# Keys and values of the memory tokens: computed in the first stage and kept in a DRAM buffer, instead of computed between the two blocks

## The reference, cut to what matters

```
def memory_mixer(q, mem, mem_norm_g, w_mem_kv):
    kv = (rmsnorm(mem, mem_norm_g) @ w_mem_kv).reshape(b, mem.shape[1], 2, MEM_HEADS, MEM_DH)
    k, v = kv[:, :, 0], kv[:, :, 1]
    ...
```

## Time and profile before

| | |
|---|---|
| median of three runs | 2339.71 us |
| the profiled execution (its span; no other time of it was kept) | 2339.5 us |
| PE busy | 2263.0 us, 97% of the span |
| DVE busy | 1471.0 us, 63% |
| ACT busy | 1038.2 us, 44% |
| POOL busy | 45.4 us, 2% |
| moved by DMA | 458.63 MB, mean 196 GB/s |
| GB/s in the first slices of 58.5 us | 367, 372, 146, 196 |
| chain that ended last | PE 86%, DVE 5%, ACT 2%, DMA 2% |

### The profile page before, as it was taken

One profiled execution on the slowest core, in us unless ns is written; L12 is line 12 of the kernel. 1 busy time (PEld: TensorE's weight loads), 2 busy tenths in 40 slices (PEclk: granted clock), 3 DMA queues, 4 the chain that ended last, 5 costly groups with the idle time before them and its releaser, 6 DMA issues.

```text
span 2339.5 us, 37594 instructions
## 1 busy us (share of the span) xinstructions
PE 2263.0 (97%) x15609; PEld 2029.3 (87%) x15609; DVE 1471.0 (63%) x2074; ACT 1038.2 (44%) x1429; POOL 45.4 (2%) x57
## 2 busy tenths in 40 slices
PE   5899999999999999989999999999999999999997
PEld 2577788899888999779999988999978998999986
DVE  3346766488476479766888855566665544576664
ACT  3134233354555643344444433444454434454444
POOL 2000000021000000000000000000000000000000
PEclk9899999999999999999999999999999999999999
DMA  9946666455444578866778756666646466644464
GB/s 367 372 146 196 219 206 200 149 151 150 126 136 127 186 243 282 290 225 198 226 248 256 228 189 190 184 181 185 184 162 192 148 192 195 175 130 131 134 198 144
DMA packets 249610, 458.63 MB, mean 196 GB/s; under 512 B 18931, under 2 KB 43825, under 8 KB 248032
## 3 DMA queue, kind: packets, MB, share of 16 engines
q1 hardware_dynamic: 246496, 442.47, 60.5%
q0 software_dynamic: 2368, 9.56, 1.1%
q10 hardware_dynamic: 576, 4.19, 0.5%
HBM read 454.07 MB, written 2.10 MB: 195 GB/s over the span
## 4 chain that ended last, share of the span: by engine, by line
PE 86%; DVE 5%; ACT 2%; DMA 2%; DVEq 2%; issue 1%; SPq 1%; ACTq 0%
PE psum L639 76%; DVE fast L1912 1%; DVE sbuf L1960 1%; DMA sbuf<-in_w_ada 1%; PE psum L616 1%; ACT fast L1315 1%; PE psum L1041 1%; PE psum L1148 1%; PE psum L710 1%; PE psum L892 1%; PE psum L947 1%; DVEq L1959 1%; PE psum L966 1%; PE psum L1178 1%; SPq L510 1%
## 5 line engine op out<-in xcount | busy, mean ns | idle before, releaser
L639 PE MATMUL psum<-fast,fast 128*128 128x256 f32 (+3 forms) x13440 | 2037.5, 312 | 19.3 <-DVE fast L1912 13.3
L639 PEld LDWEIGHTS psum<-fast,fast 128*128 128x128 f32 (+2 forms) x13440 | 1848.8, 190 | 196.8 <-issue 46.2
L1912 DVE TENSOR_TENSOR fast<-sbuf,fast 128x1024 fp32r<-128x1024 f32 (+5 forms) x685 | 784.1, 1152 | 706.8 <-ACT fast L1315 699.1
L1315 ACT ACTIVATE fast<-sbuf 128x1024 fp32r<-128x1024 f32 (+4 forms) x689 | 682.0, 997 | 1060.0 <-PE psum L639 925.0
L1960 DVE SCALAR_TENSOR_TENSOR sbuf<-sbuf,sbuf 128x512 f32<-128x512 f32 x210 | 157.8, 751 | 19.4 <-issue 1.3
L1315 ACT ACTIVATE sbuf<-psum 128x512 f32<-128x512 f32 (+5 forms) x193 | 85.6, 468 | 83.9 <-PE psum L639 37.5
L1932 DVE TENSOR_TENSOR fast<-sbuf,fast 128x512 fp32r<-128x512 f32 (+1 forms) x61 | 53.4, 876 | 4.5
L616 PE MATMUL psum<-sbuf,sbuf 128*128 128x128 f32 (+2 forms) x221 | 40.0, 291 | 11.9 <-DMA sbuf<-in_consts 9.8
L616 PEld LDWEIGHTS psum<-sbuf,sbuf 128*128 128x128 f32 (+2 forms) x221 | 27.4, 148 | 20.2 <-DMA sbuf<-in_consts 9.8
L1680 ACT ACTIVATE sbuf<-psum,sbuf 128x256 f32<-128x256 f32 x88 | 44.1, 551 | 0.0
L2334 DVE SCALAR_TENSOR_TENSOR sbuf<-psum,sbuf,sbuf 128x255 f32<-128x255 f32 x88 | 38.5, 478 | 3.3
(11 more groups left out here) (267 smaller groups left out, 982.7 us busy)
## 6 DMA issues: line engine op xcount, KB each, us to landing
sbuf<-in_w_ada SPq DMA_DIRECT2D x192, 512.0 KB, 5.0
sbuf<-in_w_up SPq DMA_DIRECT2D x176, 512.0 KB, 3.9
sbuf<-in_w_in SPq DMA_DIRECT2D x154, 512.0 KB, 3.9
sbuf<-in_w_down SPq DMA_DIRECT2D x88, 512.0 KB, 4.1
sbuf<-in_w_gate SPq DMA_DIRECT2D x64, 512.0 KB, 3.7
sbuf<-in_w_out SPq DMA_DIRECT2D x64, 512.0 KB, 4.9
sbuf<-in_w_proj_gla SPq DMA_DIRECT2D x16, 512.0 KB, 5.0
sbuf<-in_w_proj_diff SPq DMA_DIRECT2D x16, 512.0 KB, 6.1
```

Of the source, the lines that this page charges most:

```text
L639: last = mm(out, lhsT, rhs, start=first and key not in opened, stop=end, skip_group_check=True)
L1315: return A(out, in_, ACT.Copy, scale=scale)
L1912: last = tt(lo, raw, hi.bitcast(F32), ALU.subtract)
```

## The change

`km` and `vm` leave the place between the blocks. Their 16 chunks stand in the stream among the plain chunks and are multiplied behind plain chunks 8, 9, 11, 12, 14, 15, ... 29, 30 (x counts the 64 plain chunks). The memory tokens are loaded first, by ACT's queue; the tokens and the context are loaded by SP in front of its chunks 7, 9, 11 and 13. The memory units are turned behind x = 7 (three of them) and in front of the first five `km` chunks. The token transposes move to x = 23 to 27 and x = 32 to 35. The key chunks move to x = 37, 39, 42, 45, 52, 55, and two come after the last fold. The results `kmS`, `vmS` are written to the DRAM buffer `x_spill` by POOL and read back to `memback` after the first block. `norm3` has nothing beside it any more: four units at once, and the other four within the chunks of `kc`.

```
-KEYS_IN = {(3, 1): 0, (3, 5): 1, (5, 1): 2, (5, 5): 3, (7, 1): 4, (7, 4): 5}
-KEYS_AFTER = {(3, 4): 0, (3, 7): 1, (5, 3): 2, (5, 6): 3, (7, 3): 4}
-ROWS_BANK = [4, 0, 4, 6, 4, 6, 4, 6]
+MEM_AFTER = {8 + 3 * n // 2: n for n in range(16)}
+KEYS_AFTER = {37: 0, 39: 1, 42: 2, 45: 3, 52: 4, 55: 5}
+LEAD = 4
+TOKENS_AT = [7, 9, 11, 13]
+ROWS_BANK = [4, 0, 4, 0, 4, 6, 4, 6]
...
# Stream: the order of the loads
+        first = [(x, f"ada{x // 8}", ada[x // 8][x % 8], 1) for x in range(64)]
+        first += [(x - LEAD + 0.5, *memory[n], 0) for x, n in MEM_AFTER.items()]
+        first += [(x - LEAD + 0.5, "gk", gk[j], 0) for x, j in KEYS_AFTER.items()]
+        first += [(64 - LEAD + 2 * j + 0.5, "gk", gk[6 + j], 0) for j in range(2)]
+        for _, name, c, kind in sorted(first, key=lambda item: item[0]):
+            self.add(name, [c], kind)
...
# POOL
+            for b in BANKS["vm"]:
+                pool.wait_ge(S(f"bank_emptied{b}"), 2)
+            pool.dma_start(x_spill[:, 0:8, :], memS).then_inc(S("mem_moved"), 16)
...
+            pool.wait_ge(S("mem_moved"), 16)
+            pool.wait_ge(S("x1_slices"), 24)
+            pool.dma_start(memback, x_spill[:, 0:8, :]).then_inc(S("mem_moved"), 16)
...
# PE
+            def memory_chunk(n):
+                if n + 3 < 8:
+                    turn_memory(n + 3)
+                if 10 <= n < 14:
+                    turn_tokens(2 * n - 20)
+                    turn_tokens(2 * n - 19)
+                if n < 8:
+                    pe.wait_ge(S("mem_ready"), n + 1)
+                    gemm_chunk("km", n, features(1, parts_of(1)))
+                else:
+                    gemm_chunk("vm", n - 8, tokens(1, parts_of(1)))
...
+            for u in range(4):
+                turn_unit("norm3", x1T, u, 16)
+
+            def norm3_chunk(q):
+                if q in (1, 2):
+                    for u in ((4, 5) if q == 1 else (6, 7)):
+                        turn_unit("norm3", x1T, u, 16)
+                pe.wait_ge(S("norm3_ready"), min(8, (5 * q + 4) // 2 + 1))
...
# ACT, after the memory chunks
             modulate(0)
+            round_chunk(16)
+            round_chunk(17)
+            modulate(1)
+            round_chunk(18)
+            rows_copy(4)
+            round_chunk(19)
+            rows_copy(5)
+            modulate(2)
+            round_chunk(20)
+            rows_copy(6)
+            round_chunk(21)
+            rows_copy(7)
+            modulate(3)
+            for s in (22, 23, 24, 25):
                 round_chunk(s)
+            act.wait_ge(S("mem_moved"), 16)
...
# DVE, after the memory chunks
             split_tokens(0, 0)
             split_tokens(0, 1)
+            rest_chunk(16)
+            rest_chunk(17)
+            split_tokens(1, 0)
+            split_tokens(1, 1)
+            rest_chunk(18)
+            columns_keep(4)
+            rest_chunk(19)
+            columns_keep(5)
+            gains(2)
+            split_tokens(2, 0)
+            split_tokens(2, 1)
+            rest_chunk(20)
+            rest_chunk(21)
+            columns_keep(6)
+            columns_keep(7)
+            gains(3)
+            split_tokens(3, 0)
+            rest_chunk(22)
+            split_tokens(3, 1)
```

More of the change, by code:

```diff
@@ L1370, in _, with memory_unit, token_copy @@
+            def memory_unit(u):
+                act.wait_ge(S("mem_turned"), u + 1)
+                for j in range(2):
+                    k = 2 * u + j
+                    last = A(X[:, 1, 1, k, :], bank(6 + u % 2, j * T, T), ACT.Identity, scale=V("mem_norm_g_2", k))
+                last.then_inc(S("units_read"), 1)
+            def token_copy(n):
                 act.wait_ge(S("tokens_in_psum"), n + 1)
[L1371 to L1372 removed]
+                g, t = n % 8 // 2, n // 8 * 2 + n % 2
+                copy(X[:, t // 2, 1, 4 * g:4 * g + 4, P:T], bank(7).rearrange("p (a b) -> p a b", a=4)
@@ L1375, in _ @@
+            rows_copy(3)
+            for t in range(2):
+                src, emptied = filled("vm", t)
+                copy(vmS[:, t, :], src).then_inc(emptied, 1)
+            for n in range(9, 16, 2):
+                token_copy(n)
             act.drain()
@@ L2309, in row_scales @@
                 last.then_inc(S(f"{name}_scales_ready"), 1)
-            def unit(name, u, before, lc):
-                dve.wait_ge(S("units_read"), before + u + 1)
-                hi, lo = (XR[:, lc, part, 2 * u:2 * u + 2, :] for part in range(2))
-                split_values(hi, lo, X[:, lc, 1, 2 * u:2 * u + 2, :]).then_inc(S(f"{name}_ready"), 1)
             row_variance(48, 4, ("x1_squared", 8))
@@ L2318, in _ @@
             for u in range(3):
-                unit("norm2", u, 0, 0)
+                unit("norm2", u, 8, 0)
             def taps(s, i, b):
@@ L2401, in _ @@
                 pass
-            def norm3_units():
-                row_variance(48, 4, ("x1_squared", 16))
-                yield
-                row_scales("norm3", 58, "mem")
-                yield
-                for u in range(8):
-                    yield
-                    unit("norm3", u, 16, 1)
-            side = norm3_units()
-            steps("km")
-            steps("vm")
-            for _ in side:
-                pass
+            row_variance(48, 4, ("x1_squared", 16))
+            row_scales("norm3", 58, "norm2")
+            for u in range(3):
+                unit("norm3", u, 16, 1)
             def low_rank_norm(n):
@@ L2574, in _ @@
             for name, _, width in IN2:
-                steps(name)
+                if name == "kc":
+                    for q, g in enumerate(st.job[name]):
+                        rest_chunk(st.nth[g] + 2)
+                        if q in (0, 1):
+                            for u in ((3, 4) if q == 0 else (5, 6, 7)):
+                                unit("norm3", u, 16, 1)
+                        next(side, None)
+                else:
+                    steps(name)
             for k in ("uq", "ukv"):
```

350 lines of the change are left out of this document (165 added, 185 removed).

## The result

The changed kernel takes 2364.5 us (median of 4 runs, 2363.5 to 2369.4), the kernel before beside it 2340.0 us (4 runs, 2339.3 to 2341.6). The ratio is 1.0113, with an interval of 1.0101 to 1.0125: 24.6 us, or 1.1%, slower. The forecast was 2357 us within 2336 to 2370, and slower at a chance of 0.75.

The account below looks back on a forecast made before the run. The prediction had DMA setting the pace from 30 to 120 us with PE nearly full, PE the bound afterwards and, once changed, early too. Early loss and late gain summed as 2339.5 + 60.3 - 42.4 = 2357 us, range 2336 to 2370.

Parts of the forecast that it names:

- slack: First stage before, plain chunk 8 to end of `ga`: 118.0 us, 95.5 of it PE work at full clock, leaving 22.5.
- The late gain: Behind the first stage: 57.5 us taken away, 15.1 added at the bare boundary and in `kc`, net 42.4 (39.5 to 48).
- within `downb`: 8 memory units beside `downb` go, 6.5 us, and a stall of 2.51 us with slow matmuls behind it, 4.0 together.
- The nearest row: Profile row of the boundary in front of `norm2`, the same chain without cover: 14.0 us derived for `norm3`, 10.7 exposed.
- The bare norm: Second block's norm without `km` and `vm` as cover: 10.7 us exposed at the boundary plus waits in `kc`, sum 15.1.
- The four places: PE waits at x = 37, 52, 55 and after x = 63: 6.9, 6.3, 2.8 and 5.5 us, sum 21.5.
- The early side: Plain chunk 8 to end of `ga`: 143.8 + 4 + 3 + 21.5 + 6 = 178.3 us, 60.3 longer.
- half clock behind the waits: First stage, key chunks behind the four waits: the clock falls in quiet stretches, 6 us taken for four places.
- half until 41 us: Start of the first stage: PE's clock is half until 41 us, which hits the first `km` chunk, 3 us.
- Transfers: First stage stays bound by its transfers, grows by 30 us, change wins 12: 2327 us, `gv0` near 181; chance 0.12.
- Short waits: PE bound early, but waits at x = 37, 52 and 55 short since loads space plain chunks: 2337 us; chance 0.13.
- Worse: ACT and DVE make PE wait about 1 us at each of the 16 memory chunks: 2373 us; chance 0.13.

Follow-up runs that it names:

- experiment 2: Changed kernel with twelve more loads of 512 KB (6.3 MB) in the first stage, into memory that nothing reads: 2368.2 us, ratio 1.0137.
- experiment 3: Changed kernel with the 16 memory chunks multiplying one of their three pairs of matmuls, all else the same: 2348.1 us, ratio 1.0032.
- experiment 5: Changed kernel with the order of experiment 4 and key chunks behind x = 38, 40, 42, 45, 55, three after the last fold: 2344.1 us, ratio 1.0016.
- experiment 4: Changed kernel with rounding and rest of the key weights moved ahead of the quarter's halves on ACT and DVE: 2347.4 us, ratio 1.0028.
- experiment 6: Changed kernel with matmuls that feed nothing in PE's four first-stage waits: 2364.3 us with 11, 10, 4 and 8; 2362.8 us with 7, 6, 2 and 5.
- experiment 8: Experiment 5 with matmuls that feed nothing in the first stage and in front of the `norm2` and `norm3` units: 2347.6 us with 12 per boundary, 2339.1 with 6.

## Why the prediction was right, and where it was short

**The bound.** The old first stage has 22.5 us of slack over PE's work at full clock, so 48.3 us of added work must make it at least 26 us longer. Experiments 2, 3 and 5 show it from three sides: more bytes cost 4 to 7 us and not 16, less PE work helps, and with the waits nearly gone the stage is 48 us longer. The slack is not all idle time: PE's waits from 31.9 to 150 us before add up to 9.1 us, and the other 13.4 are matmuls above the prices of the sum (half clock, and short pieces). Such costs return in the changed stage, so the slack was an upper bound. In experiment 5 almost none of it is used: plain chunk 8 starts 6 us later than before, behind it PE still waits 5 us for loads and 5 us at the folds and key chunks, and the last 120 matmuls take 30.52 us instead of 27.51, 19 us in all.

**The late gain.** 42.4 us were worked out, between 39.5 and 48; the traces show 43.4 to 44.8. In front of `kc` 31.9 were expected (45.7 + 1.3 - 15.1) and 30.6 measured, within `downb` 10.5 (6.5 + 4.0) and 12.0 measured. The nearest row was the right one. The bare norm took back 45.7 + 1.3 - 30.6 = 16.4 us where 15.1 were worked out, 10.7 of them for the boundary itself.

**The waits.** The four places, 21.5 us in the sum, measured 21.6 (6.95 + 6.32 + 2.80 + 5.04 + 0.48). They follow from reading ACT's and DVE's written order against PE's place in it. Experiment 4 shows the cause by moving only that order.

**The size.** The early side came out at 68.4 instead of 60.3 us, and `gv0` started at 219.1 instead of 211. The mechanism was right, and what was mis-sized is a handful of small terms:
- plain chunk 8 starts 6.1 us later (38.01 against 31.87), where 4 were taken, and even the end from above was 5.6: +2.1;
- no term stood for waits on loads within the stage; they were 0.62 (for the weights of the first `km`), 0.21 and 2.27 us: +3.1. The last is the 64th plain chunk, whose load was issued only at 183.33 us, when a place had come free;
- half clock behind the waits was put at 6 us; against 5.68 per chunk the four places lost 2.2, 2.8, 1.6 and (against 22.0 for 96 matmuls) 1.7: +2.3;
- a `vm` chunk alternating with plain chunks takes 2.94 us, not the 2.75 of a long run: 8 x 0.19 = +1.5;
- the first `km` chunk, put at 3 us more for its clock, took 3.10 us, the full-clock time: -2.9. This was in part luck: with the same PE instructions up to there it took 3.10 us in experiment 5 too, but 4.20 in experiment 4 and 4.92 and 4.70 in the two versions of experiment 6. The forecast's "half until 41 us" was also read from durations alone: the granted clock column shows 1.00 in that stretch, before and after;
- a plain chunk that stands alone takes 0.57 us, a pair 1.00, against 0.48 each: with what else is too small to name, +2.

That is 8.1 us. The last of these and the `vm` chunk, 3.5 us, have one form: prices were read from long runs of one kind of work, and the change cuts the work into short pieces of two kinds. The others are loads (5.2 us, most of it a term put at nothing) and the clock (-0.6, two errors against each other). The late side was 1.0 us better than forecast, which hid a little of this.

**The rivals.** "Transfers" is out by experiment 2, by the DMA share (0.78 from 90 us on), and by `gv0` at 219.1 us where this rival had 181. The rule behind it, of the Trainium skill ("Perfetto Trace Analysis", Optimization Strategy), that interleaving regimes with different bounds may help, finds its two regimes here, and interleaving them lost 24.6 us: the first had less room than what was put into it. "Short waits" (2337 us) is out for the kernel as it is, since the waits came in full; as a forecast for a kernel in which they are short it was 7 us low (experiment 5, 2344). "Worse" (2373, ACT and DVE late at every memory chunk) did not happen: only the first memory chunk waited (0.62 us), and from 60 to 90 us PE is busy 30.00 of 30.00 us. POOL's write of 1 MB at 108.9 us and the read back at 1875.3 us had nobody waiting for them, as assumed.

**Still open.** A version that fills the 22.5 us of slack and no more, with only some of the 16 chunks early, was not tried: it needs the split memory tokens to stay on the chip through the first block or to be made twice. The fillers of the first stage (experiment 8) were not tried in the kernel before, so its best time may lie below 2334.9 us. And the windows show when the clock fell, not what exactly makes it fall: it did behind 2.75 us of idleness and not behind 2.62, but also behind 0.50 us where three waits for loads had gone before.

## What to carry to other kernels

A stage that is bound by its loads offers at most its length less PE's work in it at full clock (here 118.0 - 95.5 = 22.5 us, of which only 9.1 were waits); the DMA share does not tell it. Work moved there pays full price for all that goes beyond, and what it covered in its old place goes bare. When products are moved close behind what they depend on, read the written order of the other engines at that place: here 13 us by the trace, 17 by the medians, of the 25 us lost were an order on DVE and ACT that could be mended without a single instruction more. And price short alternating pieces from rows of short pieces.

## What the runs showed of the hardware

- A wait can cost PE more than its length, and short ones can do it: behind 2.75 us of idleness the granted clock was 0.50 and 32 unit matmuls took 6.72 us, behind 0.53 us (with fillers before) 3.84 at a clock of 1.00; behind 3.06 us a key chunk took 8.44 us instead of 5.7. It is not the last wait's length alone: behind 2.62 us a key chunk took 5.72, and behind 0.50 us, with three waits for loads shortly before, 120 matmuls took 30.52 instead of 27.51. The Trainium skill ("TensorE: Matmul & The Clock Gate", What's actually happening) has the slow clock as the default and activity as what lifts it; the runs with fillers agree.
- An fp32 matmul of 512 columns is two records of 0.43 us, 0.87 us in all, where a fast one of 512 columns takes 27.51 / 120 = 0.23 us: 3.8 times as long. So a count of records is not a count of instructions: the 8 matmuls of a plain chunk and of a unit are 4 in the code.
- 6.3 MB more in a stage whose DMA share was 0.95 to 1.04 for 90 us and 0.78 in the next 30 cost 4 to 7 us, not the 16 of their transfer; behind 90 us they filled time in which PE was not waiting for loads.
- Matmuls that feed nothing, 5.3 us of them in a wait of 5.9 us, made the kernel before 0.18% faster (0.08 to 0.27%). At 10.5 us in the same kind of wait they cost 4.2 us of delay and gave 2.8.
